# Loads of seven weight tiles a layer stand later among the value page loads in SyncE's queue

## What is computed

```python
h = x + W_out @ concat[ DSA(xn) * silu(g_a), DIL(xn) * silu(g_c), SSD(xn) ]
```

```python
sc = indexer_scores(qi, wi, ki_all)
_, idx = lax.top_k(sc, n_sel)
phys = jnp.take_along_axis(page_table, (pidx // page).reshape(b, -1), axis=1).reshape(idx.shape)
kv_past = pool_kv[layer, phys, pidx % page].astype(k_new.dtype)
```

## Time and profile before

| | us |
|---|---|
| median of three runs | 607.02 |
| lowest, highest | 602.06, 607.34 |
| the profiled execution, whole | 605.69 |
| its span, from first to last instruction | 603.7 |
| TensorE busy | 584.9 |
| GpSimd, VectorE, ScalarE busy | 260.1, 359.6, 168.3 |

### The profile page before, as it was taken

One profiled execution on the slowest core, in us unless ns is written; L12 is line 12 of the kernel. 1 busy time (PEld: TensorE's weight loads), 2 busy tenths in 40 slices (PEclk: granted clock), 3 DMA queues, 4 the chain that ended last, 5 costly groups with the idle time before them and its releaser, 6 DMA issues.

```text
span 603.7 us, 13968 instructions
## 1 busy us (share of the span) xinstructions
PE 584.9 (97%) x4960; PEld 413.4 (68%) x4960; DVE 359.6 (60%) x1067; ACT 168.3 (28%) x429; POOL 260.1 (43%) x464
## 2 busy tenths in 40 slices
PE   8999999999999998999999999899999999989994
PEld 7766665677777765777777665567767786657772
DVE  5864646667667774822277465556766678564224
ACT  3014332224122424621101353133411123425110
POOL 1407541476721566423300574227765137544420
PEclk9999999999889999999999999899988999999997
DMA  8979999999997799999844899999999879989997
GB/s 328 375 255 345 369 368 392 414 380 370 363 363 243 250 350 354 327 382 383 284 141 140 268 366 368 381 390 353 379 348 383 294 221 343 359 262 310 361 317 265
DMA packets 81110, 198.38 MB, mean 329 GB/s; under 512 B 12081, under 2 KB 45010, under 8 KB 80530
## 3 DMA queue, kind: packets, MB, share of 16 engines
q0 software_dynamic: 28768, 102.22, 47.9%
q1 hardware_dynamic: 52274, 95.27, 45.1%
HBM read 189.29 MB, written 52.00 MB: 400 GB/s over the span
## 4 chain that ended last, share of the span: by engine, by line
PE 83%; DMA 10%; SPq 3%; DVE 2%; issue 1%; ACT 0%; DVEq 0%; POOLq 0%; POOL 0%
PE bank L891 80%; DMA kv<-in_kk 5%; DMA kv<-in_vv 4%; PE bank L939 3%; SPq L426 2%; DMA w<-in_w 1%; DVE xn L2142 1%; SPq L422 0%; SPq L447 0%; DVE rstd L1511 0%; DVE eqs L2055 0%; DVE srow L2070 0%; DVE drow L1924 0%; DVE st4b L1929 0%; DVE pt L1876 0%
## 5 line engine op out<-in xcount | busy, mean ns | idle before, releaser
L891 PE MATMUL bank<-xn,w 128*128 128x288 f32 x1120 | 296.9, 419 | 0.3 <-DMA w<-in_w 0.3
L891 PEld LDWEIGHTS bank<-xn,w 128*128 128x128 f32 x1120 | 208.4, 193 | 71.2 <-issue 14.6
L426 POOL DMA_DIRECT2D kv<-in_kk x128 | 68.9, 539 | 116.4 <-issue 58.5
L426 POOL DMA_DIRECT2D kv<-in_vv x128 | 68.7, 537 | 59.0 <-PE bank L891 42.1
L683 ACT ACTIVATE pt<-bank 128x288 f32<-128x288 f32 x48 | 19.7, 410 | 210.6 <-PE bank L891 210.6
L891 PE MATMUL bank<-pt,kv 128*128 128x288 f32 x256 | 62.4, 406 | 0.0
L891 PEld LDWEIGHTS bank<-pt,kv 128*128 128x128 f32 x256 | 48.5, 190 | 13.4
L1592 DVE TENSOR_SCALAR_CACHE_REDUCE hit<-sc,tb 128x516 bf16<-128x516 f32 x62 | 46.5, 750 | 2.2
L891 PE MATMUL bank<-kv,pt 128*32 128x256 f32 x512 | 33.6, 384 | 4.3 <-DMA kv<-in_vv 4.2
L527 POOL DMA_DIRECT2D out_keep<-in_buf x48 | 24.4, 510 | 29.4 <-PE bank L891 27.6
L891 PE MATMUL bank<-kv,qz 128*32 128x256 f32 x512 | 35.1, 392 | 0.0
(11 more groups left out here) (253 smaller groups left out, 794.9 us busy)
## 6 DMA issues: line engine op xcount, KB each, us to landing
w<-in_w SPq DMA_DIRECT2D x70, 512.0 KB, 7.9
out_keep<-in_buf POOLq DMA_DIRECT2D x16, 1984.0 KB, 13.6
kv<-in_kk SPq DMA_DIRECT2D x128, 160.0 KB, 8.8
kv<-in_kk POOLq DMA_DIRECT2D x128, 160.0 KB, 5.9
kv<-in_vv SPq DMA_DIRECT2D x128, 128.0 KB, 4.7
kv<-in_vv POOLq DMA_DIRECT2D x128, 128.0 KB, 5.6
kv<-in_dil SPq DMA_DIRECT2D x16, 576.0 KB, 8.5
kv<-in_dil POOLq DMA_DIRECT2D x16, 576.0 KB, 7.4
```

The source lines that it names most:

```text
L426: engine.dma_start(kv[:, s, r * rec:(r + 1) * rec], a["kk" if what == "page" else "vv"][bass.ds(page + layer * N_POOL, 1)].rearrange("o p ...
L891: return pe.matmul(out, lhsT, rhs, start=start, stop=stop, skip_group_check=True, **k)
```

## The change

One line of SyncE's program changes: the seven pieces in which it goes through places 40 to 80.

```diff
@@ -491,7 +491,7 @@
                 for i in range(4):
                     consumed(*RING[32 + 2 * i:34 + 2 * i])
                     next_w(24 + i)
-                for i, (lo, hi) in enumerate(((40, 48), (48, 52), (52, 56), (56, 64), (64, 66), (66, 72), (72, 80))):
+                for i, (lo, hi) in enumerate(((40, 62), (62, 65), (65, 68), (68, 71), (71, 74), (74, 77), (77, 80))):
                     consumed(*RING[lo:hi])
                     next_w(28 + i)
                 consumed(*RING[80:])
```

## The result

| | before | after |
|---|---|---|
| median, 20 runs each, us | 604.16 | 607.65 |
| lowest to highest, us | 596.36 to 608.87 | 603.16 to 613.48 |
| ratio, 95% interval | | 1.0089 [1.0058, 1.0120] |
| profiled execution, us (span) | 605.69 (603.7) | 607.08 (605.0) |

The forecast was no change, at 606 us. The time lies inside the range of 601 to 611, but the loss of about 5 us is real: its interval excludes 1. It is of the size of one of the terms that I had cancelled against each other. That 607.65 is so near 606 is luck: the forecast started from the median of three runs, 607.02, and that of twenty is 604.16.

The account below looks back on a forecast made before the run. TensorE, 97% busy, was taken to bound the kernel, with DMA only just keeping up at value 16. From 605.69 us, minus 4.5 plus 3.9 gave 605.1, or 606 on the median's scale; range 601 to 611.

Parts of the forecast that it names:

- the terms that I had cancelled against each other: Around value 16 and tile 32: 4.5 us gained from waits removed, against 3.9 us of new waits for w32.
- What bounds the kernel, and where: TensorE busy 97% of the span; waits of 1.68 and 2.50 us ahead of value 16, and 0.35 us, would go.
- The lead of w32: w32, issued behind value 20, comes 3.06 us (first layer) and 3.03 us (second) before TensorE reaches tile 32.
- T: Time from issue to landing of w32, taken as 5.0 us, so TensorE waits 1.95 us a layer at tile 32.
- My subtraction: For w32's load: n0's 8.9 us less 4.5 us of weight-tile backlog, so 4.4 us.
- My count of what must pass: Value 20, w32, value 21 and part of 23: 3.5 loads, 5.3 us, so w32 takes 4.7 to 5.2 us.
- The upper bound: w32 takes at most 8.9 us to land, as n0 did when issued 2.4 us later into the old backlog.
- rival C: Half clock after both new waits at tile 32 adds 3.3 us, giving 608.4; chance 0.15 together with D, within 1%.
- Rival A: w32 lands as late as such loads before, near 8.9 us: 612.9 us, slower by over 1%; chance 0.09.
- rival E: The old wait at value 16 stays beside the new one at tile 32: 609.6 us; chance 0.06.
- Rival D: Value 28, value 30 or output tile 0 late by up to 2 us a layer: 607 to 609; chance 0.15 with C.
- The chances: Whole kernel: faster 0.03, same 0.88, slower 0.09; the forecast case, waits that trade places, had 0.58.

## Why the prediction was wrong, point by point

- **What bounds the kernel, and where.** Right. Both waits for value 16, and the 0.35 us at groups 6 and 7, went away when the three weight tiles left the queue ahead of them. The runs with w32 on time show the gain alone: 6.2 to 7.6 us by the means, of which 4.5 are these waits; the rest is in part a higher clock.
- **The lead of w32.** Right: 2.9 us in both layers, forecast 3.06 and 3.03.
- **T, the step that failed first.** I took 5.0 us between 3.7 and 8.9. It is 6.1 to 7.5, so the wait is 3.2 to 4.6 us a layer and not 1.95. My subtraction, 8.9 us less the 4.5 of backlog, took a backlog as the whole of the delay; value 20, directly ahead of w32, did land fast (2.8 us after its last issue), and w32 still needed 7.5. My count of what must pass gave 4.7 to 5.2 us, near the 4.1 to 4.5 at which twelve of the 16 completions were in; it took all 16 as ending together, and the last came 1.6 to 3.4 us later. A tail of 1.4 to 2.1 us is left with GpSimd's pages held, and its cause, perhaps an instruction fetch, stays open. The upper bound was not the slowest either: in the same profile w34 of the second layer took 10.9 us. With T at 6.5 the same sum gives 2 x 3.45 = 6.9 us against 4.5 us, a loss of 2.4.
- **The clock, the step that was left out.** I set it as rival C with a small chance, since no fall followed the waits of 1.68 and 2.50 us before, and the sum has it at nothing. By the following estimate it is half of the loss. The mean clock of the runs went from 0.985 to 0.980. One stretch of 3.4 us at half rate lowers the mean over 603 us by 0.0028, so there are 1.7 more of them in a run (the two profiles show one and none behind w32), at the 1.64 us of the earlier trace rows, 2.9 us. With 6.8 - 4.5 = 2.3 us of waits this is 5.2; the means of the runs in that comparison are 608.4 and 603.3 us, 5.1 apart. The same account for w32 behind value 18 gives -4.5 - 1.5 = -6.0, measured -6.2; for the three other orders with w32 on time it leaves 0.5 to 1.4 us of the gain open. For w32 behind value 22 it gives 9.9 us of waits and 5.2 of clock, 15.1, and 12.6 was measured: there 5.4 us of the half-rate stretches lie inside the waits themselves, where a slow clock costs nothing.
- **Rival A** (T near 8.9) and **rival E** (the old wait stays) did not happen; rival E does happen when w32 alone is late. **Rival D**: values 28 and 30 landed 0.8 and 0.3 us ahead of their use in the first layer, tight as feared, and were not waited for. They were in the profiled execution with w32 back in its old place, by 0.44 and 1.62 us, so this rival is real in some executions, though not the cause of the loss.
- **The chances.** The forecast of no change rested on two terms of some 4 us that were to cancel. The range held the time, but the likeliest case did not: a difference of two terms, one of them with ends 5 us apart a layer, deserved a case of its own for a loss of half a per cent to one. That the range held is no proof of the sum: it was wide enough for both terms to be off.

## What to carry to other kernels

Loads for which nobody waits are not free to be moved behind what they delay: work out the lead that is left, in us, at the new place, and hold it against the slowest comparable load under traffic, not the quickest or a mean; where they are near, one load earlier in the queue is worth more than anything gained behind it. A wait on an engine that is full otherwise can cost its length and then again in clock, here by estimate about as much, so count both, and in a wait that can't be removed idle matmuls into a bank about to be overwritten win some of it back. And a wait that lies inside the interval of a later one costs nothing: the two must be removed together.

## What the runs showed of the hardware

- Of TensorE's waits over 1.4 us in the 13 profiles, the clock fell to half at or behind those of 1.42, 2.23, 2.27, 2.30, 2.33, 2.63, 2.65, 2.95, 4.59, 7.01 and 7.40 us, and not at those of 1.52, 1.62 (twice), 1.68, 2.02, 2.50, 3.21, 3.23 or 3.59 us; at 2.12 and at 3.56 us it did once and once not. It also fell where TensorE had not waited over 0.25 us. The length of one wait doesn't tell whether it falls; the mean over many runs does tell that it costs. The waits of 7.4 and 7.0 us came with 6.8 us at half rate each, of which 2.8 and 2.6 us lie still inside the wait. The first, which ended at 245.30, and the wait itself:

```profile
242.50:249.30 6.80, 4.00 (x8) 2.86 (x9) 0.85 (x1) 0.51 (x2) 0.00 (x0) 0.50 0.73 257
237.90:245.20 7.30, 0.01 (x1) 0.00 (x0) 5.25 (x7) 1.95 (x4) 3.40 (x7) 0.81 0.90 306
```

- A load of 512 KB that shares its 16 DMA engines with one other queue took 6.1 to 7.5 us, with nothing beside it 5.0 and 5.1, and in a quiet stretch 3.7; the pages queued behind it on its own queue made no difference that shows.
- The last of a load's 16 completions can be 1.0 to 1.5 us behind the fifteenth, with the DMA engines otherwise idle.
